# A decoder trunk on one core: value products turned around into column groups of TensorE, the second output projection in two passes, and other opening loads

## What is computed

```python
# layer A
h = rms(x); a, g, mq = split(h @ w_in_a)
c = silu(layernorm(causal_dwconv(a * sigmoid(g), width 31)))
x += concat(c, mem_attend(rms(mq), mem_k[0], mem_v[0])) @ w_out_a
x += (gelu(causal_dwconv3(rms(x) @ W_g)) * (rms(x) @ W_v)) @ w_down[0]
# layer B: 6 heads, keys and values from x after layer A
k, v = split(rms_kv(x) @ w_kv); q, mq = split(rms(x) @ w_in_b)
o = softmax(q1 k1) v - lam * softmax(q2 k2) v        # per head; prompt causal
c = rms(o) * (1 - lam_init)
x += concat(c, mem_attend(rms(mq), mem_k[1], mem_v[1])) @ w_out_b
x += (the same feed-forward block)                    # w_down[1]
```

## Time and profile before

| what | value |
|---|---|
| median of three runs | 1576.59 us |
| the profiled execution, its own time | 1581.38 us |
| its span, first to last instruction | 1579.7 us |
| granted TensorE clock, mean | 0.944 |
| TensorE busy | 1463.8 us (93%) |
| VectorE busy | 956.6 us (61%) |
| ScalarE busy | 578.3 us (37%) |
| GpSimd busy | 156.1 us (10%) |

### The profile page before, as it was taken

The page is one execution under the profiler, slowest core; times in us unless marked ns, Lnnn a source line. Parts: engine busy times, 40 slices in busy tenths (PEclk is TensorE's granted clock), DMA queues, the critical chain, the costliest instruction groups (busy, mean ns, idle before and its releaser), DMA issues.

```text
span 1579.7 us, 28049 instructions
## 1 busy us (share of the span) xinstructions
PE 1463.8 (93%) x10932; PEld 1394.9 (88%) x10932; DVE 956.6 (61%) x1825; ACT 578.3 (37%) x969; POOL 156.1 (10%) x202
## 2 busy tenths in 40 slices
PE   4899876989999999999999999997899999999997
PEld 3799774789999999999988877775899999999997
DVE  4789888556663565366765455665566635653662
ACT  3444433444341222123555344444333322221222
POOL 2000103212000000000200333220110000000001
PEclk7899987789999999999999899996899999999999
DMA  7121222114233232322322333331123323233222
GB/s 208 42 66 54 88 86 70 43 53 134 87 87 92 83 94 80 94 84 67 96 81 67 108 104 105 107 94 54 53 86 89 93 81 94 82 91 90 85 74 68
DMA packets 223088, 134.88 MB, mean 85 GB/s; under 512 B 7612, under 2 KB 216209, under 8 KB 222936
## 3 DMA queue, kind: packets, MB, share of 16 engines
q1 hardware_dynamic: 215143, 111.54, 24.5%
q0 software_dynamic: 7840, 21.89, 4.7%
HBM read 126.19 MB, written 7.85 MB: 85 GB/s over the span
## 4 chain that ended last, share of the span: by engine, by line
PE 76%; DVE 14%; ACT 5%; issue 3%; SPq 1%; DMA 1%; POOL 0%; ACTq 0%; DVEq 0%; POOLq 0%
PE acc L522 58%; PE acc L699 6%; DVE conv_out L1625 3%; PE psT L957 2%; ACT w_hi L1093 1%; DVE w_lo L1528 1%; DVE softmax_stats L2016 1%; PE psX L534 1%; PE psX L893 1%; ACT exps L1391 1%; PE psX L786 1%; PE acc L534 1%; PE psT L999 1%; SPq L415 1%; PE psX L656 1%
## 5 line engine op out<-in xcount | busy, mean ns | idle before, releaser
L522 PE MATMUL acc<-xa_hi,w_hi 128*128 128x272 f32 x1760 | 371.7, 293 | 8.4 <-DVE xa_lo L1563 8.4
L522 PE MATMUL acc<-xa_hi,w_lo 128*128 128x272 f32 x1760 | 365.9, 289 | 0.0
L522 PE MATMUL acc<-xa_lo,w_hi 128*128 128x272 f32 x1760 | 364.9, 289 | 0.0
L1093 ACT ACTIVATE w_hi<-w_raw 128x1024 fp32r<-128x1024 f32 x194 | 205.4, 1059 | 378.1 <-PE acc L522 304.2
L1528 DVE TENSOR_TENSOR w_lo<-w_raw,w_hi 128x1024 fp32r<-128x1024 f32 x194 | 237.8, 1226 | 98.9 <-ACT w_hi L1093 97.4
L522 PEld LDWEIGHTS acc<-xa_hi,w_hi 128*128 128x128 f32 x1760 | 279.0, 190 | 13.6 <-issue 11.9
L522 PEld LDWEIGHTS acc<-xa_lo,w_hi 128*128 128x128 f32 x1760 | 278.5, 190 | 0.0
L522 PEld LDWEIGHTS acc<-xa_hi,w_lo 128*128 128x128 f32 x1760 | 276.6, 190 | 0.0
L522 PE MATMUL acc<-xb_hi,w_hi 128*128 128x272 f32 x896 | 197.1, 302 | 2.0 <-DVE xb_lo L1962 2.0
L522 PE MATMUL acc<-xb_hi,w_lo 128*128 128x272 f32 x896 | 187.7, 291 | 0.0
L522 PE MATMUL acc<-xb_lo,w_hi 128*128 128x272 f32 x896 | 187.2, 291 | 0.0
(11 more groups left out here) (306 smaller groups left out, 1998.0 us busy)
## 6 DMA issues: line engine op xcount, KB each, us to landing
w_raw<-in_w_up SPq DMA_DIRECT2D x88, 512.0 KB, 3.9
w_raw<-in_w_down SPq DMA_DIRECT2D x32, 512.0 KB, 3.9
w_raw<-in_w_in_a SPq DMA_DIRECT2D x14, 512.0 KB, 4.1
w_raw<-in_w_down SPq DMA_DIRECT2D x16, 384.0 KB, 3.4
w_raw<-in_w_kv SPq DMA_DIRECT2D x12, 512.0 KB, 3.9
k_pages<-in_cache_k POOLq DMA_DIRECT2D x96, 64.0 KB, 2.1
v_pages<-in_cache_v SPq DMA_DIRECT2D x96, 64.0 KB, 1.9
w_raw<-in_w_mem_kv SPq DMA_DIRECT2D x8, 512.0 KB, 3.8
```

Of the source, the lines that this page charges most:

```text
L522: last = nc.tensor.matmul(acc[slot][:, c, 0:n], w, x[:, k, c * n:(c + 1) * n], start=(k == 0 and q == 0), stop=(k == kb - 1 and q == 2))
L1093: nc.scalar.activation(whi[:, slot % 2, :], wraw[:, slot, :], ACT.Copy).then_inc(w_hi_ready, 1)
```

## The change

- Sampled tokens of a head: the weights (32 columns) are the stationary operand and the pages the moving one, four sequences at a time into four groups of 32 output partitions; VectorE copies the result (128 x 256), TensorE transposes it (new slot "OS"), and VectorE gathers the 32 columns that are wanted.
- Memory attention of the sampled tokens: the same for the product (new slot "XO" for the transposes back), and scores are made for four sequences at a time, in two goes instead of four; VectorE copies the first half and adds the second.
- Memory attention of the prompt: each head's 64 output channels in a group of their own, 128 columns for 256.
- Second output projection: two passes of eight steps of four chunks. Pass 1 takes heads 0 to 3 and runs beside head 5, in slots 160 to 191; pass 2 takes memory and heads 4 and 5. Each pass adds its own residual. The mix parts are made three slots behind each head's norm.
- Opening: x and the first weights are loaded first, the memory rows ahead of the conv state; the small parameter loads are issued by ScalarE; ScalarE scales first and squares afterwards; GpSimd's copy of the conv state is issued later.
- Sample taps: one multiply per chunk over overlapping windows, from a packed copy of the taps.

```diff
-S_FFN = (S_OUT[0] + 8, S_OUT[1] + 8)
+S_FFN = (S_OUT[0] + 8, S_OUT[1] + 16)
...
-        for j in range(4):
-            slots["GM"][j] = 30 + 10 * j
-        slots["XT"][0], slots["XV"][0] = 66, 69
+        slots["GM"][0], slots["GM"][1] = 42, 60
+        slots["XT"][0], slots["XV"][0], slots["XO"][0] = 66, 69, 71
...
+            slots["OS"][h] = v0 + 28
...
+        HALF = KD // 2
...
+        def mixed(i):
+
+            return (0, 1, 2, 3, 6, 7, 4, 5).index(i) + 8
...
-            for r, k, src, done in put:
-                if src is not None:
-                    sp.dma_start(rows[r % P:r % P + k, r // P, :], src[done:done + k, :]).then_inc(ld_rows, 16)
...
+                    load(S_OUT[l] + m, block_cols(wo, m, 0, HALF), kb=HALF)
+                    if m in (1, 3, 5):
                         value_pages(3 + m // 2)
+                for m in range(KD if l else 0):
+                    load(S_OUT[l] + KD + m, block_cols(wo, m, HALF, HALF), kb=HALF)
...
                     for mb in range(MB):
-                        last = nc.tensor.matmul(psT[:, 1, 0:2 * P], memv[:, 1, mb, c * P:(c + 1) * P],
-                                                pTt[:, mb:4:2, :], start=(mb == 0), stop=(mb == MB - 1))
+                        for x in range(2):
+                            last = nc.tensor.matmul(psT[x * MHD:(x + 1) * MHD, 1, 0:P],
+                                                    memv[:, 1, mb, c * P + x * MHD:c * P + (x + 1) * MHD],
+                                                    pTt[:, 2 * x + mb, :], start=(mb == 0), stop=(mb == MB - 1))
...
-                for b_ in range(DB):
+                for b2 in range(2):
                     for pg in range(PAGES):
-                        nc.tensor.matmul(psT[:, 1, P + b_ * DS:P + (b_ + 1) * DS], vpg[:, b_ * PAGES + pg, :],
-                                         afold[:, pg, b_ * DS:(b_ + 1) * DS], start=(b_ + pg == 0), stop=False)
-                nc.tensor.matmul(psT[:, 1, P:P + NSA], vnew[:, h, :], anew[:, :], start=False, stop=True).then_inc(at_pv, 1)
+                        for j in range(4):
+                            nc.tensor.matmul(psT[j * NSA:(j + 1) * NSA, 1, b2 * P:(b2 + 1) * P], afold[:, pg, :],
+                                             vpg[:, (2 * j + b2) * PAGES + pg, :], start=pg == 0, stop=False)
+                    for j in range(4):
+                        last = nc.tensor.matmul(psT[j * NSA:(j + 1) * NSA, 1, b2 * P:(b2 + 1) * P], anew[:, :],
+                                                vnew[:, h, :], start=False, stop=True)
+                last.then_inc(at_pv, 1)
+
+            def turn_sample(h):
+
+                pe.wait_ge(at_O, item(h, 4) + 1)
+                turn_free("OS", h)
+                for b2 in range(2):
+                    last = nc.tensor.transpose(psT[:, 0, b2 * P:(b2 + 1) * P], osam[:, b2, :], ident)
+                last.then_inc(turn_full, 1)
...
+                pe.wait_ge(turn_taken, turn_at("KM", 4 * b2 + 3) + 1)
+                pe.wait_ge(at_exp, 5 + 3 * b2)
+                for c in range(MC):
+                    for j in range(4):
+                        last = nc.tensor.matmul(psX[j * NSA:(j + 1) * NSA, 1, MEM:2 * MEM], qm2[:, c, 4 * b2 + j, :],
+                                                kTm[:, j, c * MEM:(c + 1) * MEM], start=(c == 0), stop=(c == MC - 1))
...
+                for b2 in range(2):
+                    for m in range(MB):
+                        for j in range(4):
+                            last = nc.tensor.matmul(psT[j * NSA:(j + 1) * NSA, 1, b2 * MW:(b2 + 1) * MW],
+                                                    pTt[:, m, j * NSA:(j + 1) * NSA],
+                                                    mcache1[:, 4 * b2 + j, m * MW:(m + 1) * MW],
+                                                    start=(m == 0), stop=(m == MB - 1))
...
-            for g in range(TAIL, LAST_SLOT + 1):
...
+            for m in range(KD):
+                def hooks(k, m=m):
+                    if (m, k) == (0, HALF - 1):
+                        tile_hook(S_B + 19)
+                    beside_b(TAIL + HALF * m + k)
+                mm_step(S_OUT[1] + m, m % 2, moh, mol, kb=HALF, hooks=hooks,
+                        ready=(lambda k: pe.wait_ge(cm_lo, mixed(k) + 1)) if m == 0 else None)
...
+            for m in range(2):
+                out_rest(m, range(HALF - 1))
+            for m in range(KD):
+                out_rest(m, range(HALF - 1 if m < 2 else 0, HALF))
             ffn(1, 3)
...
+                    act.dma_start(rows[r % P:r % P + k, r // P, :], src[done:done + k, :]).then_inc(ld_rows, 16)
...
+            act.wait_ge(setup_drained, PARAMS_AT + 2)
             for c in range(KD):
-                act.wait_ge(setup_drained, c + 2 + (c >= PARAMS_AT))
+                if c == PARAMS_AT:
+                    split_hi(0)
+                if c >= PARAMS_AT:
+                    act.wait_ge(setup_drained, c + 3)
+                scaled_hi(xa_hi, c, xT[:, c, :], pcol("norm_mix", c), xg_hi)
+            for c in range(KD):
+                if c == 2:
+                    split_hi(1)
                 square(xT[:, c, :])
...
+                for h in due("OV", g, 3):
+                    act.wait_ge(ov_done, h + 1)
+                    mix_part(moh[:, h, :], od[:, h, :])
...
+            for m in range(KD):
+                split_hi(S_OUT[1] + m + 2)
+                for x in range(HALF):
+                    react(TAIL + HALF * (m + 1) + x)
...
-                for t in range(DS):
-                    link(nc.vector.tensor_tensor(sprod[:, :, t, :], x[:, :, t:t + TAPS],
-                                                 w.unsqueeze(1).broadcast_to((P, DB, TAPS)), ALU.mult))
+                windows = bass.AP(x.tensor, x.offset, [list(x.ap[0]), list(x.ap[1]), [1, DS], [1, TAPS]])
+                w = taps[:, j, :].unsqueeze(1).unsqueeze(1).broadcast_to((P, DB, DS, TAPS))
+                link(nc.vector.tensor_tensor(sprod[:, :, :, :], windows, w, ALU.mult))
...
+            def sample_taken(h):
+
+                dve.wait_ge(turn_full, turn_at("OS", h) + 1)
...
+                for h in due("OV", g, 3):
+                    mix_part_lo(h, mol[:, h, :], moh[:, h, :], od[:, h, :])
...
+            dve.wait_ge(acc_free, S_B + 20)
+            for m in range(KD):
+                residual(S_OUT[1] + m, m)
+                split_lo(S_OUT[1] + m + 2)
+                for x in range(HALF):
+                    react(TAIL + HALF * (m + 1) + x)
             out_section(1, "n3", 3)
...
             pool.wait_ge(ulo_ready, FC)
+            mem_cache_v(1)
+            pool.wait_ge(ms_S, DB + 2)
             pool.memset(qpad[:, :, :], 0.0).then_inc(qp_zero, 1)
-            mem_cache_v(1)
```

More of the change, by code:

```diff
@@ L122, in build @@
         ones, _ = place("ones", [P, P])
+        taps, _ = place("taps_by_chunk", [P, CC, TAPS])
         stT, _ = place("ffn_state", [P, 2 * FC, 2 * DB])
@@ L1037, in beside_b @@
                     turn(n)
+                for h in due("OS", g):
+                    turn_sample(h)
                 for b_ in due("KM", g):
@@ L1067, in _, with out_rest @@
                 mm_step(s, s % 2, hi, lo, ready=ready, hooks=hooks)
-            for g in range(TAIL, LAST_SLOT + 1):
-                if g == TAIL + 4:
-                    tile_hook(S_B + 19)
-                beside_b(g)
-                if g == slots["S"][item(H - 1, 4)] + 1:
-                    out_part(1, 0, range(OUT_EARLY[1]))
-                if g == slots["T"][item(H - 1, 4)] + 1:
-                    out_part(1, 1, range(OUT_EARLY[1]))
-            out_section(1)
+            for m in range(KD):
[5 more added lines that the diff above has]
+                        ready=(lambda k: pe.wait_ge(cm_lo, mixed(k) + 1)) if m == 0 else None)
+            def out_rest(m, parts):
+                s = S_OUT[1] + KD + m
+                if parts[0] == 0:
+                    pe.wait_ge(w_lo_ready, s + 1)
+                    pe.wait_ge(acc_free, s - 1)
+                for i in parts:
+                    k = (2, 3, 0, 1)[i]
+                    hi, lo = (xb_hi, xb_lo) if k >= 2 else (moh, mol)
+                    if m == 0:
+                        pe.wait_ge(cm_lo, mixed(HALF + k) + 1)
+                    wh, wl = whi[:, s % 2, k * P:(k + 1) * P], wlo[:, s % 2, k * P:(k + 1) * P]
+                    for q, (w, x) in enumerate(((wh, hi), (wh, lo), (wl, hi))):
+                        for c in range(2):
+                            last = nc.tensor.matmul(acc[s % 2][:, c, 0:HT], w, x[:, HALF + k, c * HT:(c + 1) * HT],
+                                                    start=(i == 0 and q == 0), stop=(i == HALF - 1 and q == 2))
+                if parts[-1] == HALF - 1:
+                    last.then_inc(mm_done, 1)
+            for m in range(2):
+                out_rest(m, range(HALF - 1))
+            for m in range(KD):
+                out_rest(m, range(HALF - 1 if m < 2 else 0, HALF))
             ffn(1, 3)
```

(8 more changed lines are left out.)

227 lines of the change are left out of this document (113 added, 114 removed).

## The result

The changed kernel takes 1525.7 us (median of four, 1524.4 to 1526.7); the kernel before took 1576.9 (four runs, 1576.3 to 1578.5). The ratio is 0.9675 (95% interval 0.966 to 0.969): 51 us faster, where 45.8 were forecast for it (1531 us). The profiled execution took 1524.4 us, its span is 1522.7, its mean granted clock 0.965. Against the profiled execution of before it is 57.0 us shorter, so 5.8 us of what two traces show is scatter between executions. One of the 54 executions of the kernel before that were timed beside the experiments took 2390 us at a mean granted clock of 0.605; it is in no ratio.

A forecast was written before the change was run, and what follows sets the result against it. TensorE bounds layer B's memory half, nearly ties with VectorE in the convolution, sometimes waits in heads, and idles in opening and last head. 5.9 + 3.5 + 13.4 + 5 + 18 = 45.8 us off 1581.4, median 4.8 lower: 1531; range 1508 to 1553.

The forecast's parts named there:

- Opening: Start of the kernel: first matmul 5.9 us earlier from loading x and w first; bounds 2.9 and 7.9 us.
- the cover that was "used up": First projection step: GpSimd's adds of the squares, 1.6 us each from about 25, end by 34.6, just as the step does.
- Taps: Convolution chunks 2 to 5: one multiply of 1.19 us for four of 2.32; 3.5 us gained, bounds 1 and 5.
- Memory products: Layer B's memory attention: outputs 9.4 us, scores and value products 4 of 8.7; sum 13.4, bounds 7 and 17.
- Value pages in the heads: Heads 0 to 4: shorter products and no half-rate matmuls behind them, VectorE limiting the gain; 5 us in sum.
- Left over: 2.6 - 1.6 = 1.0 in heads 2, 3 and 4: Per head: VectorE's 2.6 us wait less 1.6 us of added mix-part and copy work leaves 1.0 us gained.
- all relief arrives: Rival, 15%: heads stay bound by TensorE, value pages give 22 us, memory products 17; 66 us gained, 1510 us.
- The longer idle gaps that should have cost 0.5 a head: Heads: a longer TensorE idle gap is followed by a slow stretch, taking 0.5 us off the gain.
- Tail and projection: Last head and layer B's output projection in two passes: ends at 1147.7, 18 us gained, bounds 7 and 26.
- The groups don't run side by side: Rival, 7%: products in 32-column groups don't overlap, 256 columns cost 0.46 us each; 25 us gained, 1551 us.
- The tail gives little: Rival, 17%: last head and output projection gain 7 us in place of 18; 1542 us.
- slower by half clock: Rival, 3%: TensorE gets half the clock through the heads, five heads lose 19 us each; 1626 us.

## Why the prediction was right, point by point

**Opening: the cover that was "used up" was overdrawn.** The parameters landed as forecast and earlier (copied by 16.3, not 17.5), the first matmul started at 24.1, not 25.3. But of 5.9 us only 1.6 (-0.2 to 3.3) stay where the opening is timed alone (3.7 between the traces of before and after). The step that failed is "end by 34.6, just as step 0 does, so this cover is used up". GpSimd begins at 23.8 and needs 11.3 us, not 9.6: it waits 0.77 us for the third square, which ScalarE begins only when the first add has ended, and its last five adds come every 1.81 us, not every 1.6, while VectorE writes `xa_lo` and `w_lo` beside them. The step ends at 33.1. I wrote that what comes later counts in full, and forecast no lateness; and I did not price the stretch at half clock that followed the wait in six kernels of seven. With the squares early there is no wait, and the second norm comes 6.5 us before its place with the old opening, where it came 1.4 us before. Term 5.9, measured 1.6.

**Taps: right.** Term 3.5, in the traces 3.5 to 3.6; a product of 1.19 us as read from the reduce.

**Memory products: right, a little low.** Term 13.4, measured 14.9 in the traces of before and after, 15.9 in six other kernels with the new products. The outputs gave 9.3 (9.4 forecast), with 1.93 us for four groups of four (2.1 forecast); scores and value products gave 5.7 (4 of 8.7 taken).

**Value pages in the heads: the term that was too small.** Term 5, measured 12.6 net: 4.4 up to norm 22, where 2.6 was forecast for head 1, and 1.8, 2.1 and 3.4 in heads 2 to 4, where it was 1.0 each. A quad takes 0.32 us (0.25 forecast), so the 1.92 us of a head lie above the 1.3 to 1.7 that I named as a sign, and TensorE's work falls by 3.1 us a head. The wrong step is "Left over: 2.6 - 1.6 = 1.0 in heads 2, 3 and 4": I read VectorE's 2.59 us of waiting as the room that was left until VectorE would set the pace. In the old head TensorE sets it (mix parts cost nothing there), and the new product with the clock behind it is worth 4.1 us on average (the 16.4 us between the two single-pass kernels, over four). Only then does VectorE matter, and there the second half of the step was right: the mix parts take back 1.15 us in each of three heads. The rival *all relief arrives*, with 22 for this part, was too high and the forecast too low; the truth lies midway. The longer idle gaps that should have cost 0.5 a head cost nothing: the 3.9 us of idle time in head 2 come in pieces of at most 1.0 us, and the granted clock is 1.00.

**Tail and projection: right.** Term 18, measured 20.6, of which 2.5 are the value pages of head 5. From head 4's transposed key rows (1066.43 before, 1030.06 after) I put the last norm's sum 50.6 us on and the end of the projection 81.3; they came at 49.0 and 77.8 (1107.86). Most of the difference is there before the second pass: head 5's part is multiplied at 55.8, forecast 58.6. The second pass's steps take 3.35 us (3.5 to 3.9 forecast): an `xa_lo` takes 1.34 beside GpSimd's add, not 1.84. Two passes alone are worth 16.3 us there and 10 to 14 in all, since their mix parts have to stand among the heads.

**The rivals.** *The groups don't run side by side* is shown wrong for the order as written, and true of the other order, at a higher price than I gave it. *The tail gives little* and *slower by half clock* did not happen: the clock granted from norm to norm in the heads, 0.90 to 0.95 before, is now 1.00 from norm 21 to norm 28 and 0.95 between norms 29 and 30, in the last head.

**Clock, neighbours and queues in the opening.** The Trainium skill ("TensorE: Matmul & The Clock Gate", in the section on why this matters) warns of idle gaps between bursts. The openings agree: behind a wait of 3.20 us stands a stretch at 0.50; a gap of 2.06 us went without it (0.99 and 1.00 from 30 to 42 us). The Trainium skill ("SBUF — State Buffer", in the section on who interferes with whom) says that a VectorE instruction with two inputs in SBUF contends with a GpSimd instruction that reads there. The trace agrees: four `xa_lo` take 2.87 us alone and 6.14 beside GpSimd's adds (three take 1.87 each, one falls into GpSimd's pause and takes 0.77), and an add takes 1.65 to 1.72 beside them against 1.32 where nothing runs beside it. By these rows the opening's term would have been 5.9 less a wait of 2 to 3 us, an estimate. What I drew from the Trainium skill ("DMA: Bandwidth & Descriptors", on queue arbitration), parameters 3 us late, did not come: in the trace they were copied 1.2 us before my time.

That the sum came within 5.4 us is partly luck: 4.3 too much in the opening (by the runs with it alone) against 7.6 too little in the heads, 2.6 in the tail and 1.5 in the memory part (by the traces). These make 7.4 too little; the 2 us down to 5.4 are within the scatter between traces and medians.

## What to carry to other kernels

When work is moved off the front of a chain, list what it used to be early for, and give that work's own engine and those that run beside it a duration from a row where they overlap; a cover that is exactly used up can be a wait, and the wait may cost the clock as well. In a pipeline with two engines near the bound, take the relief of the one that sets the pace in full until the other's busy time is reached, and find out which it is by adding work to one of them. Products in 32-column groups paid here only in turn over the groups, and then four cost about as much as one.

## What the hardware showed that I had not expected

- 32 products of four columns keep TensorE busy without a gap for 3.77 us, and yet the clock falls behind them: in the five microseconds that follow, it is 0.50 to 0.69 behind 41 of the 42 such products in seven kernels. With the same values as the moving operand (1.92 us, or 7.1 in the other order), it is 1.00 behind 41 of 42.
- Three products of 128 columns in one group take 0.29 us each; the same products in turn over four groups take 0.08 each.
- Work added to a tail that idles cost 3.0 us for 11.3, the granted clock of the stretch rising from 0.71 to 0.84.
